# Mixture-of-experts loop of four tiles a pass, with expert weights in six whole slots and skewed matmuls

## The reference, cut to what matters

```python
scores = jax.nn.sigmoid(t @ w_router)              # 520 x 64
idx = top 8 of 64 experts (4 of 8 groups first)    # per token
w = scores[idx] / sum * 2.5
for each expert e:  acc += gate_e * ((silu(t @ wg_e) * (t @ wu_e)) @ wd_e)   # 1024 -> 256 -> 1024
shared = (silu(t @ w_sh_gate) * (t @ w_sh_up)) @ w_sh_down
y = layernorm(ALPHA * x + g2 * (routed + shared))
```

## Time and profile before

| | |
|---|---|
| median of 3 runs | 1959.46 us (1952.16 to 1959.55) |
| the profiled execution | 1952.46 us, span 1950.6 us |
| PE, PEld, DVE, ACT, POOL busy | 86%, 53%, 33%, 21%, 16% of the span |
| mean granted TensorE clock | 0.944 of full speed |
| first and last expert matmul | 1136.9 us and 1847.9 us |
| expert weight loads | 76 of 2048 KB and 76 of 1024 KB (one of each for the shared expert) |
| gathers, scatters | 52, 50 |

### The profile page before, as it was taken

The page is one execution under the profiler, slowest core; times in us unless marked ns, Lnnn a source line. Parts: engine busy times, 40 slices in busy tenths (PEclk is TensorE's granted clock), DMA queues, the critical chain, the costliest instruction groups (busy, mean ns, idle before and its releaser), DMA issues.

```text
span 1950.6 us, 24171 instructions
## 1 busy us (share of the span) xinstructions
PE 1675.7 (86%) x8176; PEld 1041.8 (53%) x8176; DVE 639.6 (33%) x1421; ACT 408.3 (21%) x855; POOL 310.6 (16%) x571
## 2 busy tenths in 40 slices
PE   5999779988999899999969878888888888888713
PEld 2854558577857767888858633333333333333303
DVE  1213860587058842000145421111111111111186
ACT  1204431353135443000021111111111111111102
POOL 0002420255013400000001411111111111111100
PEclk8999889999999999999987989999999999999956
DMA  9113431211120083411011469999999999999681
GB/s 405 46 51 123 176 138 44 87 46 36 56 87 3 20 330 131 170 47 43 11 43 43 173 257 401 413 395 403 416 412 405 398 414 394 421 399 417 264 349 44
DMA packets 51051, 414.84 MB, mean 213 GB/s; under 512 B 5764, under 2 KB 9476, under 8 KB 23572
## 3 DMA queue, kind: packets, MB, share of 16 engines
q1 hardware_dynamic: 34276, 358.31, 46.3%
q0 software_dynamic: 14976, 54.50, 7.1%
q10 hardware_dynamic: 1728, 1.05, 0.2%
HBM read 372.91 MB, written 40.93 MB: 212 GB/s over the span
## 4 chain that ended last, share of the span: by engine, by line
PE 69%; DVE 13%; ACT 7%; issue 5%; DMA 3%; POOL 2%; ACTq 0%; SPq 0%; DVEq 0%; POOLq 0%
PE ps L1065 18%; PE ps L922 11%; PE ps L1086 10%; PE ps L883 9%; PE ps L868 7%; PE ps L954 3%; DVE work L1453 2%; DVE OA L1839 2%; ACT work L605 2%; ACT work L603 2%; DVE work L1442 1%; PE ps L839 1%; DMA W<-wq 1%; DVE work L1819 1%; PE ps L1077 1%
## 5 line engine op out<-in xcount | busy, mean ns | idle before, releaser
L1065 PE MATMUL ps<-W,work 128*64 128x512 f32 (+1 forms) x1200 | 357.0, 598 | 1.5 <-ACT work L1244 1.5
L1086 PE MATMUL ps<-work 128*64 128x512 f32 (+1 forms) x600 | 196.7, 639 | 64.1 <-ACT work L1259 64.1
L1065 PEld LDWEIGHTS ps<-W,work 128*64 128x64 f32 (+1 forms) x1200 | 129.9, 155 | 225.0 <-issue 225.0
L883 PE MATMUL ps<-Hb,W 128*128 128x260 f32 x768 | 172.9, 389 | 0.0
L883 PEld LDWEIGHTS ps<-Hb,W 128*128 128x128 f32 x768 | 148.5, 194 | 24.0 <-ACT work L1147 0.6
L1827 DVE COPY work<-ps 128x512 f32<-128x512 f32 x100 | 69.1, 691 | 269.0 <-PE ps L1086 269.0
L1086 PEld LDWEIGHTS ps<-work 128*64 128x64 f32 (+1 forms) x600 | 71.8, 163 | 157.9 <-issue 157.9
L1276 POOL TENSOR_TENSOR work<-work 128x128 f32<-128x128 f32 x168 | 82.8, 525 | 380.7 <-ACT work L605 380.3
L1250 ACT ACTIVATE work<-ps 128x256 f32<-128x256 f32 x50 | 19.2, 383 | 591.8 <-PE ps L1065 591.8
L1819 DVE TENSOR_TENSOR work<-ps,work 128x256 f32<-128x256 f32 x50 | 21.2, 424 | 358.6 <-ACT work L1250 358.6
L868 PE MATMUL ps<-W,Hb 128*128 128x512 f32 (+1 forms) x320 | 138.4, 592 | 0.0
(11 more groups left out here) (285 smaller groups left out, 2032.2 us busy)
## 6 DMA issues: line engine op xcount, KB each, us to landing
W<-wexp SPq DMA_DIRECT2D x76, 2048.0 KB, 11.8
work<-wexp SPq DMA_DIRECT2D x76, 1024.0 KB, 10.7
W<-wq SPq DMA_DIRECT2D x36, 2048.0 KB, 8.0
W<-yrows SPq DMA_DIRECT2D x6, 2048.0 KB, 16.9
work<-st_in SPq DMA_DIRECT2D x8, 1024.0 KB, 9.3
st_out<-work SPq DMA_DIRECT2D x8, 1024.0 KB, 7.1
Xb<-xT SPq DMA_DIRECT2D x2, 2080.0 KB, 17.9
work<-yrows SPq DMA_DIRECT2D x2, 2048.0 KB
```

The source lines that it names most:

```text
L883: mm = pe.matmul(ps[:, bank, 0:HALF], ring[:, q % 4, a, c, :], H[:, c, halves[b][0]:halves[b][1]], start=(c == 0), stop=(c == KC - 1))
L1065: mm = pe.matmul(ps[at, k, :], xe[:, k, c, at], GU[:, slot, c, :], start=(c == 0), stop=(c == KC - 1))
L1086: mm = pe.matmul(ps[at, 4 + hf, :], aT[:, k, f, at], WD[:, slot, f, hf * 512:(hf + 1) * 512], start=(f == 0), stop=(f == 1))
```

## The change

1. **Slots.** Five SBUF tensors become one, `room`. Six slots of 6144 columns each hold a whole expert, loaded in one transfer of 3072 KB (24 KB in a partition) on one semaphore per slot. The tiles of a pass use slots 0; 2 and 3; 1; 4 and 5.
2. **Four tiles a pass.** `MAXQ` halves; the number of passes is the number of tiles divided by four, rounded up, and the number of full tiles is twice the passes, if there are so many. Here 50 tiles become 52 in 13 passes; full and half tiles alternate as before. Tiles and halves that hold no token have an expert number too, and their weights are loaded. Each pass makes six loads, so 78 beside the shared one.
3. **Skew.** PE does, per tile t: transposes of the activations of t, `gate_up` of t+1, `turn` of t+2, down of t. The last pass stands apart, after the loop (`tiles(end, True)`). ACT, DVE and POOL follow. All loads of a tile wait for one thing, that the down matmuls of the tile that held its slots are done.
4. **Rows without a token.** Gather and scatter have a bounds check, and rows past the bound are not moved.
5. **Shared output.** Since the slots now cover its place, it is copied to `yb` and stored to `shrows` in DRAM (five stores of up to 512 KB on SP's queue) and read back before the tail (five loads), for which DVE waits (`t_back`).

```diff
-MAXQ = 34
-MAXT = 2 * MAXQ
+MAXQ = 17
+MAXT = 4 * MAXQ
...
+        GU = [view(room, EW * s, 4096, "p (c f) -> p c f", c=KC) for s in range(6)]
+        WD = [view(room, EW * s + 4096, 2048, "p (f d) -> p f d", f=2) for s in range(6)]
+        SLOTS = [(0,), (2, 3), (1,), (4, 5)]
+        SHARED = 1
...
+            def load_tile(i, k):
+                if k % 2 == 0:
+                    load_expert(i * 2 + k // 2, SLOTS[k][0])
+                else:
+                    for h in range(2):
+                        load_expert(i * 4 + (NLIST + k - 1 + h), SLOTS[k][h])
...
+            load_tile(0, 0)
+            sp.wait_ge(t_hh, 4)
+            sp.wait_ge(s_ht, 2 * TT)
+            load_tile(0, 1)
+            for t in range(TT):
+                n = min(P, NT - t * P)
+                sp.wait_ge(t_yc, 2 * t + 2)
+                sp.dma_start(shrows[t * P:t * P + n, :], yb[0:n, t % 2, :]).then_inc(t_st[t % 2], 16)
+            load_tile(0, 2)
...
+            load_tile(0, 3)
             with sp.Fori(1, nq) as i:
-                gate(sp, "sp", s_hh, i * 2 + 3)
-                load_expert(i, 0, "gu", s_gu)
-                gate(sp, "sp", s_y, i * 4 + 6)
-                load_expert(i, 0, "dn", s_dn)
...
+                for k in range(4):
+                    gate(sp, "sp", s_y, i * 8 + (2 * k + 2))
+                    load_tile(i, k)
+            gate(sp, "sp", s_add, nq * 64 + 32)
+            for t in range(TT):
+                n = min(P, NT - t * P)
+                sp.dma_start(rows_[t][0:n, :], shrows[t * P:t * P + n, :]).then_inc(t_back, 16)
...
+            def tiles(i, last):
+                for k in range(4):
+                    t = i * 4 + k
+                    gate(pe, "pe", s_a, i * 4 + (k + 3))
                     gate(pe, "pe", s_ac, t + 1)
...
+                    if not (last and k == 3):
+                        gate_up(i * 4 + (k + 1), (k + 1) % 4, i * 16 + (16 if k < 3 else 32))
+                    if not (last and k >= 2):
+                        turn(i * 4 + (k + 2), k % 2, i * 32 + 16 * ((k + 2) // 2 + 1))
+                    gate(pe, "pe", s_ac, i * 4 + (k + 2))
...
+            with pe.Fori(0, end) as i:
+                tiles(i, False)
+            tiles(end, True)
...
                 if t >= 2:
+                    act.wait_ge(t_st[t % 2], 16 * (t // 2))
...
+                    pool.indirect_dma_start(out=yrows, out_offset=bass.IndirectOffsetOnAxis(ap=ida[0:TS, k % 2:k % 2 + 1], axis=0),
+                                            in_=yb[0:TS, k % 2, :], in_offset=None, bounds_check=YTRASH - 1, oob_is_err=False).then_inc(s_add, 16)
...
+            dve.wait_ge(t_back, 16 * TT)
```

More of the change, by code:

```diff
@@ L1064, in gate_up @@
                     for at, slot in parts(k):
-                        mm = pe.matmul(ps[at, k, :], xe[:, k, c, at], GU[:, slot, c, :], start=(c == 0), stop=(c == KC - 1))
+                        mm = pe.matmul(ps[at, k % 2, :], xe[:, k % 2, c, at], GU[slot][:, c, :], start=(c == 0), stop=(c == KC - 1))
                 mm.then_inc(s_hh, 1)
[L1068 to L1074, removed]
+            def tiles(i, last):
+                for k in range(4):
+                    t = i * 4 + k
+                    gate(pe, "pe", s_a, i * 4 + (k + 3))
@@ L1252, in _, with tiles @@
             take_x(0, 0)
-            with act.Fori(0, nq) as i:
-                for k in range(2):
-                    silu(i * 2 + k, k)
-                    take_x(i * 2 + (k + 1), 1 - k)
-                    gate(act, "act", s_at, i * 2 + (k + 1))
-                    gate(act, "act", s_y, i * 4 + (2 * k + 6))
-                    act.activation(aT[:, k, :, :].rearrange("p f n -> p (f n)"), ps[:, 2, 0:2 * P], ACT.Copy).then_inc(s_ac, 1)
+            def tiles(i, last):
+                for k in range(4):
+                    gate(act, "act", s_at, i * 4 + (k + 1))
+                    gate(act, "act", s_y, i * 8 + (2 * k + 6))
+                    act.activation(aT[:, k % 2, :, :].rearrange("p f n -> p (f n)"), ps[:, 2, 0:2 * P], ACT.Copy).then_inc(s_ac, 1)
+                    if not (last and k == 3):
+                        silu(i * 4 + (k + 1), (k + 1) % 2)
+                    if not (last and k >= 2):
+                        take_x(i * 4 + (k + 2), k % 2)
+            silu(0, 0)
+            take_x(1, 1)
+            with act.Fori(0, end) as i:
+                tiles(i, False)
+            tiles(end, True)
             layer_norm_act(act, 1)
@@ L1819, in gated, with tiles @@
                 dve.tensor_tensor(av[:, k, :], ps[:, k, FE:2 * FE], sg[:, k, :], ALU.mult).then_inc(s_a, 1)
-            with dve.Fori(0, nq) as i:
-                for k in range(2):
-                    gated(i * 2 + k, k)
-                    gate(dve, "dve", s_add, i * 32 + (16 * k + 16))
-                    for hf in range(2):
-                        gate(dve, "dve", s_y, i * 4 + (2 * k + hf + 9))
-                        dve.tensor_copy(yb[:, k, hf * 512:(hf + 1) * 512], ps[:, 4 + hf, :]).then_inc(s_yc, 1)
+            def tiles(i, last):
+                for k in range(4):
+                    if not (last and k == 3):
+                        gated(i * 4 + (k + 1), (k + 1) % 2)
+                    gate(dve, "dve", s_add, i * 64 + (16 * k + 16))
+                    for hf in range(2):
+                        gate(dve, "dve", s_y, i * 8 + (2 * k + hf + 9))
+                        dve.tensor_copy(yb[:, k % 2, hf * 512:(hf + 1) * 512], ps[:, 4 + hf, :]).then_inc(s_yc, 1)
+            gated(0, 0)
+            with dve.Fori(0, end) as i:
+                tiles(i, False)
+            tiles(end, True)
+            dve.wait_ge(t_back, 16 * TT)
             def total(m):
```

150 lines of the change are left out of this document (72 added, 78 removed).

## The result

The changed kernel takes 2033.35 us (median of 4 runs, 2028.09 to 2036.3), the kernel before 1958.87 us (4 runs on the same chip). The ratio is 1.0394, with a 95% interval of 1.0375 to 1.0413: slower by 75 us. The forecast was 1917 us, 35 less than the profiled execution before; the profiled execution after takes 2028.09 us. The page of the kernel after, for the earlier trace rows: its span, granted clock and DMA by slices, and its chain that ended last.

What follows compares the result with a forecast made beforehand. The weight stream on the DMA was taken to bound the loop: PE ends at 1809.3 us, plus 102.7 and 3.5 of tail gives 1915.5 of span, plus 1.9 around it 1917.4 us; range 1888 to 1952.

Steps and rivals of the forecast that it cites:

- What is late next is the weights, and the loop becomes bound by the DMA: Expert loop: 5.37 MB a tile at 410 GB/s, 13.1 us a tile; chance 0.54, time 1917 us.
- Both of the prediction's own signs of being wrong: Expert loop: its DMA rate falls under 400 GB/s, or PE waits for anything but weights.
- the forecast pace of 26.2 us: Expert loop: two tiles in 26.2 us, a sign that the forecast is right.
- the forecast's times leave 632 (1161 to 1793): Expert loop: load for tile 4 issued at 1161 us, last weights landing at 1793 us.
- Chain of scatters: Rival, software queue: each scatter waits for the one before; 14.2 us landing gives 15.4 us a tile, 2026 us; chance 0.08.
- Against it: fewer rows: Scatter landing: argument against the scatter rival; with the 62% of real rows, landing is 10.2 us instead of 14.2.
- skipped rows save nothing: Rival, gathers and scatters: 5.77 MB a tile, loop ends 18 to 38 us later, 1935 to 1955 us; chance 0.14.
- The skew: PE in the loop: both waits go, 1.85 us a tile, for two more tiles, 24 us; PE alone 12.04 us a tile.
- The rate: DMA in the loop: 410 GB/s taken, so 254 MB of remaining loads take 620 us.
- The start: Before the loop: load of slot 1 ahead of the first gather adds 2 us (0 to 8); first `gate_up` at 1139.
- the tail: After PE's last: reading back 2.1 MB of `shrows` adds 3.5 us (0 to 7) to 102.7 us.
- Code loading: Rival, PE loop: body grows from 12 to 24 KB and returns must load code, about 1990 us; chance 0.05.

Runs made afterwards that it cites:

- experiment 12: Changed kernel, 24 KB loads kept, gather of t+4 issued as soon as turn t+2 has read its rows, before the wait for scatter t-1: 1970.07 us.
- experiments 1: Changed kernel with each expert loaded in three transfers of 8 KB in a partition instead of one of 24 KB: 1939.18 us, ratio 0.9904.
- experiment 2: Changed kernel with each expert loaded in two transfers, 16 and 8 KB in a partition, instead of one of 24 KB: 1935.76 us, ratio 0.9886.
- experiment 5: Changed kernel with each expert load cut by partitions into two of 64, pieces still 24 KB in a partition: 2524.82 us, ratio 1.2904.
- experiment 3: Changed kernel without the bounds checks; rows without a token gathered from zeros and scattered to trash rows: 2042.03 us.
- experiment 7: Changed kernel loading only gate and up weights (16 KB in a partition), down weights left out, output not the reference's: 1860.76 us, ratio 0.9518.

## Why the prediction was wrong

- **"What is late next is the weights, and the loop becomes bound by the DMA" is the step that failed.** Late next is the gather: a ring of two tiles, 19.3 us of landing and 11.5 us of work, 15.4 us a tile. Both of the prediction's own signs of being wrong came: the loop's rate is 350 GB/s, under 400, and PE waits for something else than weights. The ring stood in the kernel before too, and could have been summed there: 11.2 us, then `turn`, transposes, copy and down (7.0 us, 1428.83 to 1435.82), and some 4 us of VectorE and GpSimd as in the chain after (1418.3 to 1422.3), about 22 us, under the 27.8 us of two tiles. I never priced the landing of the gather. In the new order the work is 9.0 us at the full clock (11.5 less 2.5: 0.9 on `turn`, 1.6 on down), so at the forecast pace of 26.2 us the ring closes from a landing of about 17 us on, an estimate from these numbers. Two tiles took 4.5 us more than 26.2: about 2 of them are landing beyond 17 us, and about 2.5 the low clock behind the wait. The error in size: from the third `gate_up` to the last it is 743.5 us (1159.66 to 1903.14), 15.2 a tile, where the forecast's times leave 632 (1161 to 1793).
- **The cause of the long landing was named in a rival, with too small a chance.** "Chain of scatters" (0.08) said that rows wait among weight packets and that these double from 24 KB on; its 14.2 us without saved rows, 15.4 us a tile and 2026 us came close (13.0, 15.4 and 2033). That it came so close is luck, since its ring was the second and not the first: with the gather's ring open it gives 14.1 us a tile and 1970 us (experiment 12). The first is the gather's, because it lies in the same queue behind the scatter and pays the turns of both. The Trainium skill ("DMA: Bandwidth & Descriptors", Queues, rings and completion order) says that an engine takes the queues with work in turn, a whole packet from each. The trace agrees in the main: 303 software packets with 343 of the weights during one landing, and landings that follow the packet length in experiments 1, 2 and 5, and hardly the bytes of the rows in experiment 3.
- **"Against it: fewer rows" was wrong.** The landing was scaled by the 62% of real rows; the skipped rows still go out as packets (146.8 for each transfer, with the check and without), and saved 9 us in all. The rival "skipped rows save nothing" was right on the packets and wrong on what they cost.
- **The skew** does what it should: both waits of the earlier trace rows are gone, and alone it gives 11.7 us a tile on PE (12.0 forecast, experiment 7).
- **The rate** was right once the queue runs: 405 and 408 GB/s in experiments 1 and 2 for 410. There PE ended at 1831.8 and 1827.3 us, 18 to 23 us after the forecast's 1809.3: 13.2 us a tile for 13.1 accounts for some 5 to 7, a first `gate_up` at 1142.3 for 1139 for 3, and the rest wasn't separated.
- **The start** was 2.4 us early, **the tail** 4.7 us longer for 3.5 forecast: VectorE starts 11.1 us after the first load, about 3 more than I allowed.
- **Code loading** didn't occur: no instruction packet shows between 1200 and 1800 us.

## What to carry to other kernels

Before transfers are made larger, find every small transfer that shares the engines with them: each of its rows can wait for one packet of the large one, so its landing grows with packet length times rows per engine, its own bytes aside. Then put this landing into each ring of the program (from landing back to the issue of the next one) and compare it with the pace; a ring that was slack by some 6 us becomes the bound, and the engines are then full for a part of it only. Here 16 and 8 KB in a partition in place of 24 KB, with everything else of the change kept, gives 1935.76 us, 1.1% under the kernel before.

## What the runs showed of the hardware

- **Two queues share the engines nearly packet by packet**: during a landing of 19.3 us 303 packets of the gathers and scatters passed with 343 of the weight queue (rows of 24 KB), during one of 12.5 us 288 with 338 (rows of 16 and 8 KB, experiment 2).
- **A row skipped by the bounds check is not free**: 15264 packets on the software queue with the check and without it; 14 MB fewer in 600 us gave 9 us.
- **Loads to 64 of 128 partitions run at half the rate**: 217 GB/s at a share of 0.99, for 405 to 408 with 128 partitions. The Trainium skill ("SBUF — State Buffer", Door 1: The DMA port swizzle, and "DMA: Bandwidth & Descriptors", The descriptor swizzle) puts partitions 0 to 63 on half of the 16 ports. By the 435.2 GB/s that the Trainium skill ("DMA: Bandwidth & Descriptors", Where 436 GB/s comes from) gives for all ports an estimate is 217.6; experiment 5 agrees.
- **A pause on PE costs twice**: behind a wait of 4.7 us the next two groups took 1.94 and 5.26 us for 1.10 and 3.65, at a granted clock of 0.50 and 0.69; `turn` took 1.94 us behind all five such waits between 1411 and 1535 us. Over 1200 to 1800 us the granted clock was 0.89, for 0.98 before. A group can also run low without such a wait, as the down group at 1446.14, 5.35 us behind a wait of 1.37.
- **The length of the weight packets hardly changed the rate** (405 GB/s with 8 KB, 408 with 16 and 8 KB); it was the latency of the other queue that changed (gathers after 10.2 and 12.5 us).
